# Turning softmax weights by VectorE squares and DMA in two more branches of a hybrid attention layer

## The reference, cut to what matters

```python
proj = h @ w_in                       # h: RMS-normed x, 1024 x 1024
# a: forgetting attention, 8 heads of 64: softmax(q k / 8 + c[t] - c[s]) @ v
# b: sparse attention, 8 heads sharing k and v; top 256 keys by an indexer; ALiBi
# c: dilated windows, 12 heads in 3 groups (128,1), (512,4), (2048,16); ALiBi
logits = jnp.where(kpos[None, :] <= qpos[:, None], logits, -jnp.inf)
p = jax.nn.softmax(logits, axis=-1)
o = jnp.einsum('bhqk,bkhd->bqhd', p, v)
...
merged = sigmoid(ga)*(ya @ w_a) + sigmoid(gb)*(yb @ w_b) + sigmoid(gc)*(yc @ w_c)
return x + merged @ w_o
```

## Time and profile before

| | |
|---|---|
| median of 3 runs | 1348.22 us (1348.14 to 1348.27) |
| the profiled execution | 1348.53 us, its span 1346.7 us |
| TensorE busy | 1326.0 us, 98% of the span |
| VectorE, ScalarE, GpSimd busy | 771.0, 629.4, 264.1 us |
| stages c, a (until the last channel's attention) | 130 to 396 us, 610 to 777 us |

### The profile page before, as it was taken

How to read it: one execution, slowest core, us unless ns; L and a number is a source line. 1 busy time by engine, 2 the same in 40 slices (tenths; PEclk the granted TensorE clock), 3 DMA queues, 4 the chain that set the end, 5 groups by cost and what they waited for, 6 DMA issues and landing times.

```text
span 1346.7 us, 20780 instructions
## 1 busy us (share of the span) xinstructions
PE 1326.0 (98%) x7690; PEld 1082.1 (80%) x7690; DVE 771.0 (57%) x1716; ACT 629.4 (47%) x1381; POOL 264.1 (20%) x423
## 2 busy tenths in 40 slices
PE   7999999999999999999999999999999999999998
PEld 6988888777878888887788777787878788888886
DVE  6569866766766875565555555744445354233534
ACT  7467766766754541113443465644454322213223
POOL 3123211002103100003344313323332220000000
PEclk9999999999999999999999999999999999999999
DMA  7054222122214322225555423433544352222522
GB/s 227 24 141 126 71 63 72 50 53 73 72 41 119 99 64 82 80 72 163 162 153 155 141 87 105 127 92 84 156 127 124 119 161 55 78 78 63 188 100 96
DMA packets 146052, 139.54 MB, mean 104 GB/s; under 512 B 13888, under 2 KB 124096, under 8 KB 145696
## 3 DMA queue, kind: packets, MB, share of 16 engines
q0 software_dynamic: 22896, 67.42, 16.9%
q1 hardware_dynamic: 97824, 58.22, 16.0%
q10 hardware_dynamic: 25232, 12.59, 3.2%
HBM read 99.95 MB, written 34.03 MB: 99 GB/s over the span
## 4 chain that ended last, share of the span: by engine, by line
PE 95%; DVE 2%; ACT 1%; issue 1%; POOL 1%; DMA 0%; ACTq 0%; POOLq 0%; DVEq 0%
PE bank L1118 23%; PE bank L1120 23%; PE bank L1119 23%; PE bank L1291 6%; PE slot L1252 6%; PE bank L1264 5%; PE slot L1118 2%; PE slot L1119 2%; PE slot L1120 2%; PE slot L1226 1%; PE bank L1131 0%; DVE slot L1871 0%; ACT yc L1554 0%; DMA iq_st<-iq_hl 0%; PE bank L1177 0%
## 5 line engine op out<-in xcount | busy, mean ns | idle before, releaser
L1118 PE MATMUL bank<-hs,w_hl 128*128 128x512 f32 x1088 | 431.5, 397 | 0.7 <-DVE qa L1814 0.7
L1120 PE MATMUL bank<-hs,w_hl 128*128 128x512 f32 x1088 | 424.3, 390 | 0.0
L1119 PE MATMUL bank<-hs,w_hl 128*128 128x512 f32 x1088 | 423.8, 390 | 0.0
L1651 DVE TENSOR_TENSOR w_hl<-w_raw,w_hl 128x512 fp32r<-128x512 f32 (+1 forms) x168 | 113.6, 678 | 220.7 <-ACT w_hl L1355 219.2
L1120 PEld LDWEIGHTS bank<-hs,w_hl 128*128 128x128 f32 x1088 | 204.2, 188 | 44.0
L1118 PEld LDWEIGHTS bank<-hs,w_hl 128*128 128x128 f32 x1088 | 204.3, 188 | 43.6 <-issue 3.4
L1119 PEld LDWEIGHTS bank<-hs,w_hl 128*128 128x128 f32 x1088 | 204.6, 188 | 39.6
L1355 ACT ACTIVATE w_hl<-w_raw 128x512 fp32r<-128x512 f32 (+1 forms) x168 | 103.9, 621 | 165.1 <-PE bank L1120 155.9
L1678 DVE TENSOR_SCALAR_CACHE_REDUCE idle_out<-score,state 128x768 uint8<-128x768 f32 (+3 forms) x140 | 115.0, 822 | 4.0
L1871 DVE CUSTOM_DVE_ANT_0 slot<-slot,score 128x128 f32<-128x128 f32 (+5 forms) x64 | 47.0, 786 | 50.1 <-PE slot L1252 50.0
L1560 ACT ACTIVATE idle_out<-score,state 128x896 bf16<-128x896 f32 x64 | 69.9, 1093 | 10.0 <-DVE state L1674 8.8
(11 more groups left out here) (338 smaller groups left out, 2415.1 us busy)
## 6 DMA issues: line engine op xcount, KB each, us to landing
w_raw<-in_w_in_dram SPq DMA_DIRECT2D x136, 256.0 KB, 2.9
merged_scratch<-ms POOLq DMA_DIRECT2D x16, 512.0 KB, 3.5
ms<-merged_scratch POOLq DMA_DIRECT2D x16, 512.0 KB, 4.0
square_scratch<-pb ACTq DMA_DIRECT2D x20, 256.0 KB, 2.3
xn<-in_x_dram SPq DMA_DIRECT2D x8, 512.0 KB, 6.6
iq_st<-iq_hl POOLq DMA_DIRECT2D x32, 128.0 KB, 2.8
w_raw<-in_w_o_dram SPq DMA_DIRECT2D x16, 256.0 KB, 4.0
v_scratch<-vtc POOLq DMA_DIRECT2D x6, 512.0 KB, 3.1
```

The costliest lines, as they stand in the source:

```text
L1118: pe.matmul(out_, wh, mh, start=start, stop=False)
L1119: pe.matmul(out_, wh, ml, start=False, stop=False)
L1120: return pe.matmul(out_, wl, mh, start=False, stop=stop)
L1651: v.tensor_tensor(lo, src, hi.bitcast(F32), ALU.subtract).then_inc(w_low, 1)
```

## The change

In c head 0 of each run but the last is turned by squares and DMA instead of by PE, and in a both heads of the 17 runs that had squares already. c had 140 pieces turned by PE, now 72; a had 188, now 88. So 168 transposes of PE are gone (L1264), with the copies of 47 groups by ScalarE (L1537: 151 before, 104 after). Added are 23 + 17 VectorE transposes, 23 + 17 stores issued by ScalarE, and 92 + 68 loads issued by POOL. The ring for PE's turned pieces in c has two places instead of four, and the freed memory holds c's squares. a's second pair of square buffers lies in part where PE's turned pieces of a lie; ScalarE's copies of the remaining turns wait for the last square's `pv`.

In c the exp of both heads stays together. VectorE's transpose comes behind the `bit` step, and ScalarE's store directly behind the exps, before weights, banks or counts. In a the second head's transpose waits for its exp, and ScalarE's second store stands right behind the first.

```diff
-SQUARED = {"a": 8, "b": 4}
-LAG = {"a": 3, "b": 2}
-PTS = {"c": 4, "a": 4, "b": 3}
+SQUARED = {"c": 4, "a": 8, "b": 4}
+HEADS = {"c": 1, "a": 2, "b": 1}
+LAG = {"c": 2, "a": 3, "b": 2}
+PTS = {"c": 2, "a": 4, "b": 3}
...
-        by_dma = [br == "b" and br in SQUARED or br == "a" and r[0]["ch"] + 1 < NCH["a"] and runs[s + 1][0]["ch"] + 1 < NCH["a"]
+        by_dma = [br == "c" and s + 1 < n or br == "b" and br in SQUARED or br == "a" and r[0]["ch"] + 1 < NCH["a"] and runs[s + 1][0]["ch"] + 1 < NCH["a"]
...
+                own = [[(x["b"], hh, c) for x in runs[s] for c in range(x["W"] // P)] for hh in range(HEADS[br])]
+                goal, second = goals[len(squares) % 2], sum(y["br"] == "a" for y in squares)
+                goals[len(squares) % 2] += 64 * HEADS[br]
...
                 plan.append(("exp", runs[s][-1]))
+                if by_dma[s] and br == "a":
+                    step("square_second", unit=runs[s][-1])
+                elif br == "a":
+                    for x in runs[s]:
+                        x["behind"] = squares[-1]
...
             elif x["br"] == "c":
                 pick(now=False)
+                for f in moving:
+                    f()
+                if moving:
+                    step("square_store", unit=runs[s][-1])
+                moving.clear()
                 pump(2 * rate)
...
+            def load_square(u, hh):
+                n, nb = u["square"], u["wide"] // P
+                for j in range(4):
+                    pool.dma_start(PTQ[u["br"]][n % 2][hh][32 * j:32 * j + 32, 0:nb, :].rearrange("a b (i c) -> a (b i) c", i=4),
+                                   square_dram[n % 2 + 2 * hh][0:nb, :, 32 * j:32 * j + 32].rearrange("b (i a) c -> a (b i) c", i=4)
+                                   ).then_inc(square_in[n % 2], 16)
...
+                elif kind == "square_second":
+                    pool.wait_ge(second_stored, 16 * (a["unit"]["second"] + 1))
+                    load_square(a["unit"], 1)
...
-                            pe.wait_ge(square_in[a["square"] % 2], 64 * (a["square"] // 2 + 1))
+                            pe.wait_ge(square_in[a["square"] % 2], a["goal"])
...
+            def store_square(u, hh):
+                n, W = u["square"], u["wide"]
+                if hh:
+                    act.wait_ge(squared_second, u["second"] + 1)
+                else:
+                    act.wait_ge(squared, n + 1)
+                if u["room"]:
+                    act.wait_ge(square_in[n % 2], u["room"])
+                act.dma_start(square_dram[n % 2 + 2 * hh][0:W // P].rearrange("b p c -> p b c"),
+                              PR[u["br"]][:, hh, 0:W].rearrange("p (b c) -> p b c", c=P)
+                              ).then_inc(second_stored if hh else square_stored, 16)
...
+                elif kind == "square_second":
+                    u = a["unit"]
+                    own = PR[u["br"]][:, 1, 0:u["wide"]]
+                    dve.wait_ge(slot_free, last_slot(u) + 1)
+                    v.transpose(own, own).then_inc(squared_second, 1)
```

More of the change, by code:

```diff
@@ L238, in open_parts @@
             return 2 * own - len(runs[r][0]["moved"]) if by_dma[r] else 16
+        moving = []
         defer[0] = True
@@ L273, in square @@
                     return
-                own = [(x["b"], 0, c) for x in runs[s] for c in range(x["W"] // P)]
+                own = [[(x["b"], hh, c) for x in runs[s] for c in range(x["W"] // P)] for hh in range(HEADS[br])]
+                goal, second = goals[len(squares) % 2], sum(y["br"] == "a" for y in squares)
+                goals[len(squares) % 2] += 64 * HEADS[br]
                 at = len(squares) - 2
                 for x in runs[s]:
-                    x.update(square=len(squares), single=sum(y["slots"] == 1 for y in squares),
-                             moved={part: k for k, part in enumerate(own[:SQUARED[br]])})
-                step("square", unit=runs[s][-1], n=len(squares), before=squares[at] if at >= 0 else None)
+                    x.update(square=len(squares), single=sum(y["slots"] == 1 and y["br"] != "c" for y in squares),
+                             moved={part: k for parts in own for k, part in enumerate(parts[:SQUARED[br]])},
+                             wide=min(len(own[0]), SQUARED[br]) * P, room=goal, goal=goal + 64 * HEADS[br], second=second)
+                if br != "c":
+                    step("square", unit=runs[s][-1], n=len(squares), before=squares[at] if at >= 0 else None)
+                else:
+                    moving.append(lambda: step("square", unit=runs[s][-1], n=runs[s][0]["square"],
+                                               before=squares[at] if at >= 0 else None))
                 squares.append(runs[s][-1])
@@ L629, in hybrid_layer_kernel @@
         PT = {br: at(k, f"pt{br}", [P, PTS[br], 4, P]) for br, k in (("c", 54), ("a", 36), ("b", 40))}
-        PTQ = {"a": [at(k, f"ptsa{k}", [P, TB, P]) for k in (44, 76)], "b": [at(46, "ptsb", [P, 4, P])]}
+        PTQ = {"c": [[at(k, f"ptsc{k}", [P, 4, P])] for k in (58, 60)], "a": [[at(k, f"ptsa{k}", [P, TB, P]) for k in pair] for pair in ((36, 40), (44, 76))], "b": [[at(46, "ptsb", [P, 4, P])]]}
         idle_out, ties = at(96, "idle_out", [P, T], BF16), at(96, "ties", [P, T], F16)
@@ L1496, in _ @@
                               ).then_inc(bias_ready, 1)
-                elif kind == "square":
+                elif kind == "square" and a["unit"]["br"] != "c":
                     u = a["unit"]
@@ L1500, in _ @@
                         act.wait_ge(square_stored, 16 * a["n"])
-                    if u["held"] is not None and any(part[1] == 0 for part in u["held"]["groups"][0]["parts"]):
+                    if u["held"] is not None and any(part[1] == 0 for grp in u["held"]["groups"][:1] for part in grp["parts"]):
                         full(act, u["held"]["groups"][0]["use"])
@@ L1511, in _ @@
                     if a["held"] is not None:
-                        full(act, a["held"]["groups"][-1]["use"])
-                        if a["held"]["dma"] and not a["dma"]:
+                        for grp in a["held"]["groups"][-1:]:
+                            full(act, grp["use"])
+                        if a["held"]["dma"] and a["br"] == "a":
+                            act.wait_ge(second_stored, 16 * (a["held"]["second"] + 1))
+                        if a["held"]["dma"] and (not a["dma"] or a["br"] == "c"):
                             act.wait_ge(square_stored, 16 * (a["held"]["square"] + 1))
-                    for hh in range(1 if a["dma"] else 0, 2):
+                    for hh in range(1 if a["dma"] and a["br"] != "c" else 0, 2):
                         act.wait_ge(logit_ready, a["L"][hh] + 1)
@@ L1536, in _ @@
                         turned_room(act, grp)
+                        if u["br"] == "a":
+                            full(act, u["behind"]["pv"])
                         A(PT[u["br"]][:, grp["tp"] % PTS[u["br"]], 0:n, :].rearrange("p c q -> p (c q)"), bank[b][:, 0:n * P],
```

35 lines of the change are left out of this document (16 added, 19 removed).

## The result

The changed kernel takes 1366.12 us (median of 4 runs, 1365.33 to 1366.77), the one before 1348.18: 1.0132 times as long, 95% interval 1.012 to 1.0144. The prediction was 1346.7 with a range of 1335 to 1355. It is slower by 17.9 us where a small gain was forecast, and 11 us beyond the range's end.

The account below looks back on a forecast made before the run. PE, busy 98% of the span, was taken as the bound. Savings less waits gave -0.1 us in c and -1.4 in a, so -1.5 against 1348.53: 1347.0 profiled, 1346.7 as a median, range 1335 to 1355.

Parts of the forecast that it names:

- PE is the bound, and 22.35 us leave its list: PE's turns in c and a: removed pieces save 11.05 us in c and 11.3 in a, together 22.35.
- c's second half of q and first half of k, 6.95 lost and 4.0 hidden: Bank copies in c come late: 4.75 us lost at q, 2.2 at k; 4.0 of the savings become waiting.
- -0.1: Net for c: -7.05 + 4.75 + 2.2 us.
- the cover holds: Rival: bank delays don't reach PE; -18.3 us, 1330, or 1338 with half of the delays; chance 0.27.
- a's second half of q, +1.95, +0.95, +0.95: Three runs in a: second transpose and store delay the bank copy; 3.8 us in all, 0.9 of savings hidden.
- contention +1, between 0 and 6: Landing times in a as DMA share goes from 0.56 to some 0.85: +1 us; upper end 0.4 in 14 runs.
- +3.0 for the last square: a's last square: POOL issues four more loads behind the four, so `pv` starts 3.0 us later.
- 0.5 for the slots: a's slots: logits that wait for the exps of the run before cost 0.5 us more.
- 0.9 + 0.75 hidden: Savings in a that show up as waiting: 0.9 us at second halves of q, 0.75 at the last square.
- The slower rival: Landings too late in a's runs stop PE at `pv` and ScalarE at stores: 14 runs x 0.8, 1358; chance 0.20.
- The sign that it gave at `pv`: In a: `pv` rows with DMA waits of 0.8 and more through 630 to 770, `ptsa` landings over 5, time near 1358.

Follow-up runs that it names:

- the kernel with both kinds and no added waits: Kernel before plus 17 more stores and 68 more loads in a, loads taken from the input so POOL waits for no added landing: 1355.41 us (1.0049).

## Why the prediction was wrong

*PE is the bound, and 22.35 us leave its list*: nearly. The turns gave 8.6 in c and 10.5 in a, and in a 0.75 more but for the lower clock (11.3 predicted). PE's busy time fell by 9.8 us and not by some 20, one reason being that slower matmuls count as busy. c's remaining turns take 9.7 instead of 7.2, mostly because in the first channel VectorE is late with v too (`vtc`, 1.4), a place I had not listed.

*c's second half of q and first half of k, 6.95 lost and 4.0 hidden*: right. 10.95 predicted, 10.7 measured, and the copy at 190.93 for 190.85. That c came out at +2.1 and not at -0.1 is the turns' 2.4. The step was then put to the test by moving one instruction, and 12.7 us came back. The rival "the cover holds" failed for c as it was written, and holds for c once the store is behind the copy (10.5 of 11.05 arrive).

*a's second half of q, +1.95, +0.95, +0.95*: the first is right (0.74 to 2.63). The two others measured 1.57 and 3.69. In both, the first store stands until loads have landed, and most of all in the last, where the transposes alone would have let it go 2.5 us earlier.

*The failed step* is a's part of the sum, in the term "contention +1, between 0 and 6", together with +3.0 for the last square and 0.5 for the slots, and in a term that the sum did not have, PE's clock. For all of a's waits, hidden savings included, the sum had 9.95 us (3.8 + 3.0 + 0.5 + 1, and 0.9 + 0.75 hidden). Measured were some 21 us of waiting and some 7 of lower clock. The traffic alone cost 7.1 (the kernel with both kinds and no added waits), above my upper bound, with 5.2 of it waiting; with everything that waits on it the second head's transfers cost 23. The share was forecast well (0.85, measured 0.86). The size put to it was not: I took the median landing of one kind of load at 0.56 for what it would be at 0.85. The runs show next to nothing lost at 0.70 and 0.75 and seven us at 0.87, since landings grow and the slack in front of them is used up. The last square's term was 3.0 for POOL's four more loads behind a start at 766.50; PE waited 3.13 and 5.10 at the last two, since the last one's stores were issued late, behind a landing, and took 5.7 and 9.0 to land. The slots' 0.5 measured 4.2. The clock was put at nothing without a reason: the sum reckoned with the full clock of the rows of before.

*The slower rival* named the mechanism and the place: landings beyond 5.1 us, a store that stops ScalarE with copies and exps behind it. It said 1358 with 14 runs at 0.8. It was right in kind and short in size: the loss is not spread over 14 runs but stands in five waits of 1.5 to 3.7 and two at the end. The sign that it gave at `pv`, waits of 0.8 and more all through 630 to 770, did not show: `pv` waits 0.3 at most there, and landings come out at ScalarE, where stores and exps wait for them. Its 1358 is nearer than the forecast, but by a price that the runs do not bear out. It had a chance of 0.2, and its upper side was cut from the range. The ends of the range were taken from sums with contention as a small term, so the case in which it is the largest was priced too low.

The Trainium skill, "DMA: Bandwidth & Descriptors", section "Issuing engines are not separate DMA queues", says that transfers started by different engines run on the same 16 DMA engines. The trace agrees: SP's weights went from 3.1 to 6.2 us while only ScalarE's and POOL's transfers were added. It was cited beside the rival. It should have been weighed in the sum.

That VectorE's added transposes fit beside PE's work, a's run without transfers (which has no second store on ScalarE either) and c's with the late store show: -9.3 and -10.5 us. As far as these runs tell, what a lacks is DMA time.

## What to carry to other kernels

Before work is moved from a busy engine to DMA, add up the DMA share of the stage after the move, and try the bare traffic on the old kernel: two kinds of transfer that cost 0.6 and 1.1 us one at a time cost 7 together. Where an instruction must wait (a store for its transpose), put it behind the copies that free a bank for the bounding engine; the place of one store in the list was worth 12.7 us in c. In a, where landings were late, the same move gained 1.0 us, less than the noise. Look at how much later a landing may come before anything waits for it, most of all at the last item of a pipeline, which here has one run less of lead and the longest wait. And reckon with the clock where the bounding engine is TensorE: a wait can cost more than its length.

## What the runs showed of the hardware

- Landing times grow with the share. From 610 to 777 us the weights' loads, 256 KB each, take 3.1 us (median) at a share of 0.56, 4.0 at 0.61 (a without the second head's transfers), 4.2 at 0.70, 4.3 at 0.75, and 6.2 to 6.6 at 0.86 and 0.87 in the changed kernel and in the two with both kinds of added traffic.
- A store of 448 KB lands in 3.7 us at 0.56 and in 5.7 at 0.86 (medians). The longest, 9.0, is one issued 0.47 us behind another of its size.
- Idle stretches of PE of 3.13 and 5.10 us, with 1.65 us of work between them, went with a granted clock of 0.50 from 784 to 792 us (0.77 in the 4 us before), which made the waits 2.3 us dearer than they are long. Single waits of 2.63 and 3.69 were followed by a stretch at 0.50 as well, and so was one of 1.52 (at 664), while one of 2.71 (at 721) was not.
- With the DMA engines at 0.86 to 0.88, runs of one kernel differ by 1.4 to 8 us, at 0.75 by 5; those of the kernel before mostly stay within some tenths.
